# Attention with the inverse sums folded into the matrix that turns the probabilities, multiplied in float32

## The chip, the core and the metric

The kernel runs on one core of a Trainium2 chip. TensorE (PE in the rows, with its weight loads as PEld) multiplies matrices, VectorE is DVE, ScalarE is ACT, GpSimd is POOL, and SyncE (SP) issues transfers. The metric is the device time of one execution in microseconds (us), the median of several runs.

## What is computed

One layer of a hybrid decoder on 1024 positions of width 1024: a gated feed-forward block, a mixer with two branches (a recurrence and an attention), and a second feed-forward block. The change touches only the attention, whose core is this, for 8 heads and queries in blocks of 128:

```python
def attend(i):
    start = i * Q_BLOCK
    qn = lax.dynamic_slice_in_dim(q_nope, start, Q_BLOCK, axis=1)
    qr = lax.dynamic_slice_in_dim(q_rope, start, Q_BLOCK, axis=1)
    sc = jnp.einsum('bqhd,bkhd->bhqk', qn, k_nope) + jnp.einsum('bqhr,bkr->bhqk', qr, k_rope)
    sc = sc.astype(jnp.float32) * scale
    causal = k_idx[None, :] <= (start + jnp.arange(Q_BLOCK))[:, None]
    sc = jnp.where(causal[None, None], sc, -jnp.inf)
    p = jax.nn.softmax(sc, axis=-1).astype(v.dtype)
    return jnp.einsum('bhqk,bkhd->bqhd', p, v)
```

## The kernel before

Every large product is made of three matmuls on operands that are split into a high part and a low part (`mm3`, lines 88 to 90; ScalarE makes the high part at line 94, VectorE the low part at line 98). In the trace these operands stand as f32 or fp32r.

The attention works through 64 steps n, eight query tiles s = 0 to 7 for each of eight heads h. Step n has the scores of 128 queries against the (s + 1) x 128 keys that they may see. Every engine has its own instruction queue, written out in the order of the steps, and semaphores tie the queues together:

- `scores` (TensorE): three matmuls for each piece of up to 512 keys and one bfloat16 matmul that adds the causal mask (line 2245). Scores of step n go to one of two pairs of PSUM banks, so scores n wait for the exponentials of step n - 2.
- `maximum` (VectorE, line 2256) and `exponent` (ScalarE, line 2266, which also leaves the row sum in `rs`). The exponentials go to one of three buffers of `probs`.
- `normalise` (GpSimd): line 2272 raises the 128 sums to the power -1, and line 2275 multiplies the whole of `prob(n)`, 128 x (s + 1) x 128, by them in place.
- `turn` (TensorE, line 2290) transposes the s + 1 blocks of 128 x 128 of `prob(n)` through the identity into PSUM bank 4 (the first four blocks, piece 0) and bank 5 (the others, piece 1). The program calls it two steps late: the queue has scores n and then turn n - 2. There is one bank for each piece, so `turn` of a step waits until VectorE has taken the same piece of the step before (`pt_split`).
- `turned_hi` (ScalarE, line 94) and `turned_lo` (VectorE, line 98) split the turned blocks into `a_pt`.
- `product` (TensorE, line 2322) multiplies the turned probabilities by the values once for four query tiles. ScalarE (`take`, line 2338) and VectorE (`add`, line 2343) bring the result into `a_o`.
- Beside steps 1 and 7 of even heads, and 1, 3, 6 and 7 of odd heads, a `unit` projects the queries or keys of a later head (`unit_of`, 9 or 6 matmuls of 512 columns, rows `ps<-cq,w` and `ps<-ckv,w`). VectorE multiplies two parts of a query unit by the rotation's tables (lines 2188 and 2189) and splits the rest (2191), GpSimd adds the two parts (`rope_pool`, line 2207, in its queue behind `normalise` of the step), ScalarE takes the sum (line 2175), and its exponentials of the next step stand behind that in its queue.

A head has 1 + 2 + ... + 8 = 36 blocks to turn, so the kernel turns 288. The work repeats with a period of two heads, since the units differ for even and odd heads; scores of even heads have 96 rows, those of odd heads 128.

Of the kernel before, what the change touches and what calls it, by code (L numbers as in the profile page):

```python
# [19 lines left out]
ALU = mybir.AluOpType  # L20
# [3 lines left out]
P = 128  # L24
# [27 lines left out]
BASE = 16512  # L52
# [4 lines left out]
AT_AREA = AT_U + 65536  # L57
# [6 lines left out]
class Core:  # L64


    def __init__(self, nc, ctx):
        self.nc, self.ctx = nc, ctx
        self.ps = ctx.enter_context(nc.psum_tensor("ps", [P, 8, HALF], F32))
        self.squared = None  # L70
# [166 lines left out]
class TileNorm:  # L237
# [118 lines left out]
    def turn(self, pe, t, b, bank_free=None):  # L356
        pe.wait_ge(self.S["gained_r"], self.pres + t + 1)
        if bank_free is not None:
            pe.wait_ge(self.S["u_split"], self.split_count(bank_free))
        for k in range(DK):  # L360
            last = pe.transpose(self.c.ps[:, b + k // 4, (k % 4) * P:(k % 4 + 1) * P],  # L361
                                self.work(t)[:, k * P:(k + 1) * P], self.c.ident[:, :])
        last.then_inc(self.S["turned"], 1)
# [1616 lines left out]
class Attention:  # L1980
# [6 lines left out]
    def __init__(self, c, w, lat, w_uq, w_ukv):  # L1987
        self.c, self.nc, self.w, self.lat = c, c.nc, w, lat
        names = ("v_done", "v_hi", "v_lo", "zero", "kr_hi", "kr_split", "kr_copied", "unit_done", "q_hi", "q_rot", "q_sum", "rope_hi", "q_split",
                 "k_hi", "u_dve", "s_done", "max_done", "p_done", "norm_done", "t_done", "pt_hi", "pt_split", "o_done",  # L1990
                 "o_aux", "o_add", "o_hi", "o_split")
        self.S = {n: c.sem("a_" + n) for n in names}
        vq = w_uq.rearrange("(k p) (h e) -> p k h e", p=P, h=HEADS)
        vkv = w_ukv.rearrange("(k p) (h e) -> p k h e", p=P, h=HEADS)
        self.n_v = w.new(KC * HEADS * VH)
        for k in range(KC):
            w.piece(self.n_v, w.raw_of(self.n_v)[:, k * HALF:(k + 1) * HALF].rearrange("p (h e) -> p h e", e=VH),
                    vkv[:, k, :, NOPE:NOPE + VH])
        self.n_a = []
        half = ROPE // 2  # L2000
        for h in range(HEADS):
            n = w.new(QC * P + (0 if h % 2 else KC * P))
            q = w.raw_of(n)[:, 0:QC * P].rearrange("p (k f) -> p k f", f=P)
            even = ((0, QK, 0), (QK, half, NOPE + half), (QK + half, half, NOPE))
            odd = ((0, half, NOPE + half), (half, half, NOPE), (ROPE, ROPE, NOPE), (NOPE, NOPE, 0))
            for to, width, at in odd if h % 2 else even:
                w.piece(n, q[:, :, to:to + width], vq[:, :, h, at:at + width])
            if h % 2 == 0:
                for k in range(KC):
                    w.piece(n, w.raw_of(n)[:, (QC + k) * P:(QC + k + 1) * P].rearrange("p (h e) -> p h e", e=NOPE),  # L2010
                            vkv[:, k, h:h + 2, 0:NOPE])
            self.n_a.append(n)
        u = AT_U
        self.pt_hi, self.pt_lo = (c.at(u + 16384 * i, f"a_pt{i}", [P, 8, 4, P], F32R) for i in range(2))
        self.q_hi, self.q_lo = ([c.at(u + 32768 + 4096 * (2 * par + i), f"a_q{par}{i}", [P, SEQ], F32R) for par in range(2)]
                                for i in range(2))
        k_at = (u + 49152, u + 57344, AT_AREA + 73728)
        self.k_hi, self.k_lo = ([c.at(at + 4096 * i, f"a_k{n}{i}", [P, SEQ], F32R) for n, at in enumerate(k_at)] for i in range(2))
        self.v = c.at(AT_AREA + 40960, "a_v", [P, HEADS, NT, P], F32R)
        self.rot, self.rot2 = c.at(AT_AREA + 81920, "a_rot", [P, HALF]), c.at(AT_AREA + 100352, "a_rot2", [P, HALF])  # L2020
        self.probs = c.at(AT_AREA + 83968, "a_probs", [P, 3, SEQ])
        self.o = c.at(AT_AREA + 96256, "a_o", [P, SEQ])
        self.o_lo3 = c.at(AT_AREA + 36864, "a_o_lo3", [P, SEQ], F32R)
        self.neg, self.rs, self.inv = (c.at(BASE + 2400 + 64 * i, f"a_s{i}", [P, 16]) for i in range(3))
        self.scale = float(QK) ** -0.5

        self.units = [("q", 0, 0), ("k", 0, 0), ("q", 0, 1), ("k", 0, 1)]
        for h in range(HEADS - 1):
            if h % 2:
                self.units += [("k", (h + 1) // 2, 0), ("q", h + 1, 0), ("k", (h + 1) // 2, 1), ("q", h + 1, 1)]  # L2030
            else:
                self.units += [("q", h + 1, 0), ("q", h + 1, 1)]
        self.index = {unit: i for i, unit in enumerate(self.units)}
        self.closes = [self.index[("k", 0, 1)]] + [self.index[("q", h, 1)] for h in range(1, HEADS)]
# [231 lines left out]
        self.nc.scalar.activation(self.prob(n), self.seen(n), ACT.Exp, bias=self.neg[:, i:i + 1], scale=1.0,  # L2266
                                  accum_out=self.rs[:, i:i + 1]).then_inc(self.S["p_done"], 1)

    def normalise(self, pool, n):
        i = n % 16  # L2270
        pool.wait_ge(self.S["p_done"], n + 1)
        self.nc.gpsimd.tensor_tensor(self.inv[:, i:i + 1], self.rs[:, i:i + 1], self.c.expo[:, 1:2], ALU.pow)\
            .then_inc(self.S["norm_done"], 1)
        pool.wait_ge(self.S["norm_done"], 2 * n + 1)
        self.nc.gpsimd.tensor_scalar(self.prob(n), self.prob(n), self.inv[:, i:i + 1], 1.0, ALU.mult, ALU.mult)\
            .then_inc(self.S["norm_done"], 1)

    def turn(self, pe, n):
        c, s = self.c, n % HEAD_TILES
        pe.wait_ge(self.S["norm_done"], 2 * n + 2)  # L2280
        if n == 0:
            pe.wait_ge(self.S["u_dve"], 4)
        for b in self.pieces(n):
            if b == 0 and n > 0:
                pe.wait_ge(self.S["pt_split"], self.piece(n - 1, 0) + 1)
            if b == 1 and n >= HEAD_TILES or b == 1 and s > 4:
                pe.wait_ge(self.S["pt_split"], self.piece(n - 1 if s > 4 else n - 5, 1) + 1)
            for j in range(4 * b, min(4 * b + 4, s + 1)):
                at = s - j if b else j
                last = pe.transpose(c.ps[:, 4 + b, at * P:(at + 1) * P], self.prob(n)[:, j * P:(j + 1) * P], c.ident[:, :])  # L2290
            last.then_inc(self.S["t_done"], 1)

    def turned(self, x, n, b):
# [105 lines left out]

    def pool_step(self, pool, n):  # L2400
        if n > 0 and self.beside(n - 1):
            pool.wait_ge(self.S["norm_done"], 2 * n)
            self.rope_pool(pool, self.beside(n - 1))
        self.normalise(pool, n)

    def pe_step(self, pe, n):
        h, s = n // HEAD_TILES, n % HEAD_TILES
# [236 lines left out]
def hybrid_layer(nc, a, out):  # L2644
# [6 lines left out]
    with ExitStack() as ctx:  # L2651
# [47 lines left out]
        with nc.Block() as block:  # L2699
# [522 lines left out]
            def _(pe):  # L3222
# [8 lines left out]
                for q in range(NT):  # L3231
                    turn(f1, q)
# [77 lines left out]
                for g in range(3):  # L3310
                    for k in range(DK - 2):
                        op.chunk_of(pe, g, k)
                        if g > 0:
                            for s, q in out_steps(g, k):
                                if s == 5:
                                    if q == 0:
                                        op.evacuated(pe, 1)
                                    turn(f2, q)
                    op.tail_of(pe, g)
                turn(f2, 5)  # L3320
                op.evacuated(pe, 6)
                turn(f2, 6)
# [31 lines left out]
```

## Time and profile before

| | us |
|---|---|
| median of 3 runs | 2243.08 |
| lowest and highest | 2242.76 and 2245.47 |
| the profiled execution, its own time | 2243.93 |
| its span in the trace | 2242.1 |
| TensorE busy in the span | 2152.5 (96%) |
| VectorE, ScalarE, GpSimd busy | 1368.2, 979.4, 405.5 |
| the 64 steps of the attention in it | from 1244 to 1456 |

The profiled execution's own time is 1.8 us above its span, and its span covers first to last instruction. Times in rows are in microseconds from the start of the span, unless a column says ns. Matmuls are pipelined: the duration of one contains its latency, and what a further one costs is the distance between two starts.

### The profile page before, as it was taken

Reading aid. Unit: us, or ns where it says so; the run is one execution under the profiler, and the core shown is the slowest. Engines: PE = TensorE matmul, PEld = TensorE weight load, DVE = VectorE, ACT = ScalarE, POOL = GpSimd, SP = SyncE. Lnnn points to the kernel's source line nnn. Section 1 sums busy time; section 2 is a strip of 40 time slices with the busy share of each in tenths; the row PEclk is TensorE's granted clock in tenths of the full one; section 3 lists DMA queues with packets and bytes.
Section 4 is the critical chain, followed back from the end, with each engine's and each line's share of the span. In section 5 each row is a group of like instructions: output and inputs, shape, how many; then the busy total and the mean of one; then the engine's idle time right before and its main releaser. Section 6 shows DMA issues by size and latency. Waiting matters only on the chain.

```text
span 2242.1 us, 25934 instructions
## 1 busy us (share of the span) xinstructions
PE 2152.5 (96%) x9837; PEld 1787.4 (80%) x9837; DVE 1368.2 (61%) x1719; ACT 979.4 (44%) x1559; POOL 405.5 (18%) x444
## 2 busy tenths in 40 slices
PE   5999999999998999999999888899899999999998
PEld 4888788878886888888888677788788888888886
DVE  7667865557585665311212788677856766547666
ACT  6443333334362777411323666535533333333444
POOL 3123320000032122000011455402213331000012
PEclk9999999999999999999999999999999999999999
DMA  3355442252442211222411100255335453216234
GB/s 122 95 171 188 154 165 71 71 202 94 151 159 80 52 48 47 66 76 69 124 44 38 29 10 10 104 194 209 105 98 192 166 192 126 69 50 230 94 137 155
DMA packets 220293, 249.85 MB, mean 111 GB/s; under 512 B 24261, under 2 KB 161546, under 8 KB 220170
## 3 DMA queue, kind: packets, MB, share of 16 engines
q1 hardware_dynamic: 220170, 248.19, 33.7%
q8 instruction: 79, 1.29, 0.2%
q14 instruction: 44, 0.36, 0.1%
HBM read 192.06 MB, written 55.57 MB: 110 GB/s over the span
## 4 chain that ended last, share of the span: by engine, by line
PE 88%; DVE 5%; ACT 2%; issue 2%; POOL 1%; DMA 0%; SPq 0%; POOLq 0%; ACTq 0%; DVEq 0%
PE ps L88 29%; PE ps L89 28%; PE ps L90 28%; PE ps L2322 1%; PE ps L2290 1%; PE ps L361 1%; POOL a_rot L2207 1%; ACT a_probs L2266 1%; DVE a_pt L98 0%; DVE a_s L2256 0%; DVE entry_y L346 0%; DVE a_rot L2189 0%; DVE a_rot L2188 0%; DMA entry_x<-in_x_dram 0%; ACT w_hi L94 0%
## 5 line engine op out<-in xcount | busy, mean ns | idle before, releaser
L98 DVE TENSOR_TENSOR ff_w_lo<-ff_raw,ff_w_hi 128x512 fp32r<-128x512 f32 x264 | 211.7, 805 | 172.5 <-ACT ff_w_hi L94 172.1
L89 PE MATMUL ps<-ff_t,ff_w_hi 128*128 128x512 f32 x704 | 273.9, 389 | 0.0
L90 PE MATMUL ps<-ff_t,ff_w_lo 128*128 128x512 f32 x704 | 273.9, 389 | 0.0
L88 PE MATMUL ps<-ff_t,ff_w_hi 128*128 128x512 f32 x704 | 273.9, 389 | 0.0
L94 ACT ACTIVATE ff_w_hi<-ff_raw 128x512 fp32r<-128x512 f32 x264 | 164.7, 627 | 177.4 <-PE ps L90 172.7
L88 PE MATMUL ps<-d_b_hi,d_a_hi 128*128 128x512 f32 x608 | 237.5, 391 | 3.8 <-DVE d_a_lo L98 3.7
L90 PE MATMUL ps<-d_b_hi,d_a_lo 128*128 128x512 f32 x608 | 236.6, 389 | 0.0
L89 PE MATMUL ps<-d_b_lo,d_a_hi 128*128 128x512 f32 x608 | 236.6, 389 | 0.0
L98 DVE TENSOR_TENSOR w_lo<-w_raw,w_hi 128x1024 fp32r<-128x1024 f32 (+2 forms) x81 | 90.5, 1119 | 235.0 <-ACT w_hi L94 235.0
L88 PE MATMUL ps<-ff_b,ff_w_hi 128*128 128x512 f32 x528 | 208.5, 395 | 6.0 <-ACT ff_u2x L696 5.0
L89 PE MATMUL ps<-ff_b,ff_w_hi 128*128 128x512 f32 x528 | 207.7, 393 | 0.0
L90 PE MATMUL ps<-ff_b,ff_w_lo 128*128 128x512 f32 x528 | 207.5, 393 | 0.0
L88 PE MATMUL ps<-u_hi,w_hi 128*128 128x512 f32 x512 | 200.8, 392 | 2.4 <-DVE u_lo L98 2.4
L89 PE MATMUL ps<-u_lo,w_hi 128*128 128x512 f32 x512 | 200.2, 391 | 0.0
L90 PE MATMUL ps<-u_hi,w_lo 128*128 128x512 f32 x512 | 200.1, 391 | 0.0
L88 PEld LDWEIGHTS ps<-ff_t,ff_w_hi 128*128 128x128 f32 x704 | 132.3, 188 | 27.6
L89 PEld LDWEIGHTS ps<-ff_t,ff_w_hi 128*128 128x128 f32 x704 | 132.2, 188 | 27.5
L90 PEld LDWEIGHTS ps<-ff_t,ff_w_lo 128*128 128x128 f32 x704 | 132.2, 188 | 27.3
L94 ACT ACTIVATE w_hi<-w_raw 128x1024 fp32r<-128x1024 f32 (+2 forms) x81 | 78.3, 968 | 152.6 <-PE ps L90 145.2
L88 PEld LDWEIGHTS ps<-d_b_hi,d_a_hi 128*128 128x128 f32 x608 | 114.2, 188 | 29.4 <-DVE d_a_lo L98 6.1
L90 PEld LDWEIGHTS ps<-d_b_hi,d_a_lo 128*128 128x128 f32 x608 | 114.1, 188 | 23.8
L89 PEld LDWEIGHTS ps<-d_b_lo,d_a_hi 128*128 128x128 f32 x608 | 114.2, 188 | 23.3
(301 smaller groups left out, 4312.1 us busy)
## 6 DMA issues: line engine op xcount, KB each, us to landing
ff_raw<-in_ffn_w_gate_dram SPq DMA_DIRECT2D x44, 512.0 KB, 3.9
ff_raw<-in_ffn_w_up_dram SPq DMA_DIRECT2D x44, 512.0 KB, 3.9
d_sums<-in_ffn_w_down_dram SPq DMA_DIRECT2D x44, 512.0 KB, 4.1
sums_scratch<-d_sums SPq DMA_DIRECT2D x88, 256.0 KB, 2.6
w_raw<-in_w_in_dram SPq DMA_DIRECT2D x32, 512.0 KB, 4.0
d_raw<-sums_scratch SPq DMA_DIRECT2D x24, 512.0 KB, 3.2
w_raw<-in_w_out_dram SPq DMA_DIRECT2D x24, 512.0 KB, 3.9
spill_scratch<-ff_st SPq DMA_DIRECT2D x44, 256.0 KB, 3.0
```

Source lines behind the costliest of these rows:

```text
L88: pe.matmul(out, lh, rh, start=start, stop=False, skip_group_check=go_on)
L89: pe.matmul(out, lh, rl, start=False, stop=False, skip_group_check=go_on)
L90: return pe.matmul(out, ll, rh, start=False, stop=stop, skip_group_check=go_on)
L94: return nc.scalar.activation(hi, src, ACT.Copy)
L98: return nc.vector.tensor_tensor(lo, src, as_f32(hi), ALU.subtract)
L361: last = pe.transpose(self.c.ps[:, b + k // 4, (k % 4) * P:(k % 4 + 1) * P], self.work(t)[:, k * P:(k + 1) * P], self.c.ident[:, :])
L2207: self.nc.gpsimd.tensor_tensor(self.rot[rope, :], self.rot[rope, :], self.rot2[rope, :], ALU.add)\
L2266: self.nc.scalar.activation(self.prob(n), self.seen(n), ACT.Exp, bias=self.neg[:, i:i + 1], scale=1.0, accum_out=self.rs[:, i:i + 1]).then ...
L2290: last = pe.transpose(c.ps[:, 4 + b, at * P:(at + 1) * P], self.prob(n)[:, j * P:(j + 1) * P], c.ident[:, :])
L2322: last = pe.matmul(c.ps[:, 6, first * P:HALF], self.v[:, h, j, :], pt[:, unit, first:4, :].rearrange("p b q -> p (b q)"), start=j + i == 0 ...
```

## The change

GpSimd no longer touches the exponentials. It multiplies the 128 x 128 identity by the inverse sums, which gives a diagonal matrix (`shares`, three buffers in turn). TensorE then turns the unscaled exponentials by an ordinary matmul against that diagonal in place of a transpose against the identity. `prob(n)` stays the operand that is loaded as weights, and the diagonal is the one that streams. Both are float32 and the new instruction is `pe.matmul`, not `pe.transpose`. The semaphore `norm_done`, raised twice in a step, becomes `inv_done` and `share_done`, each raised once. `turn` waits for `share_done`.

```diff
-    def normalise(self, pool, n):
+    def share(self, pool, n):
         i = n % 16
         pool.wait_ge(self.S["p_done"], n + 1)
         self.nc.gpsimd.tensor_tensor(self.inv[:, i:i + 1], self.rs[:, i:i + 1], self.c.expo[:, 1:2], ALU.pow)\
-            .then_inc(self.S["norm_done"], 1)
-        pool.wait_ge(self.S["norm_done"], 2 * n + 1)
-        self.nc.gpsimd.tensor_scalar(self.prob(n), self.prob(n), self.inv[:, i:i + 1], 1.0, ALU.mult, ALU.mult)\
-            .then_inc(self.S["norm_done"], 1)
+            .then_inc(self.S["inv_done"], 1)
+        pool.wait_ge(self.S["inv_done"], n + 1)
+        self.nc.gpsimd.tensor_scalar(self.shares[n % 3][:, :], self.c.ident[:, :], self.inv[:, i:i + 1], 1.0, ALU.mult, ALU.mult)\
+            .then_inc(self.S["share_done"], 1)
 
     def turn(self, pe, n):
...
-        pe.wait_ge(self.S["norm_done"], 2 * n + 2)
+        pe.wait_ge(self.S["share_done"], n + 1)
...
-                last = pe.transpose(c.ps[:, 4 + b, at * P:(at + 1) * P], self.prob(n)[:, j * P:(j + 1) * P], c.ident[:, :])
+                last = pe.matmul(c.ps[:, 4 + b, at * P:(at + 1) * P], self.prob(n)[:, j * P:(j + 1) * P], self.shares[n % 3][:, :], start=True, stop=True)
```

The order on the engines stays. On TensorE, at the first two steps of an odd head, the queue before has the last score matmuls of step 0 of that head, the turn of tile 6 of the head before, the scores of step 1, the turn of tile 7, and then a unit:

```order
L2245 MATMUL ps<-mask_b,ident_b 128x128
L2290 MATMUL ps<-ident,a_probs 128x128 x7
L88 MATMUL ps<-a_k_172,a_q_167 128x256
L89 MATMUL ps<-a_k_175,a_q_167 128x256
L90 MATMUL ps<-a_k_172,a_q_169 128x256
L2245 MATMUL ps<-mask_b,ident_b 128x128
L2290 MATMUL ps<-ident,a_probs 128x128 x8
L88 MATMUL ps<-ckv_106,w_hi 128x512
```

The same place in the changed kernel, where line 2292 is the new matmul:

```order
L2246 MATMUL ps<-mask_b,ident_b 128x128
L2292 MATMUL ps<-a_shares_186,a_probs 128x128 x7
L88 MATMUL ps<-a_k_172,a_q_167 128x256
L89 MATMUL ps<-a_k_175,a_q_167 128x256
L90 MATMUL ps<-a_k_172,a_q_169 128x256
L2246 MATMUL ps<-mask_b,ident_b 128x128
L2292 MATMUL ps<-a_shares_187,a_probs 128x128 x8
L88 MATMUL ps<-ckv_106,w_hi 128x512
```

Nothing moved there; only the kind of the 7 and 8 instructions and their streamed operand are different. On GpSimd, at the end of an even head, the queue before is this (`a_s_184` are the inverse sums):

```order
L2275 TENSOR_SCALAR a_probs<-a_probs,a_s_184 128x896
L2272 TENSOR_TENSOR a_s_184<-a_s_183,expo 128x1
L2275 TENSOR_SCALAR a_probs<-a_probs,a_s_184 128x1024
L2207 TENSOR_TENSOR a_rot<-a_rot,a_rot_178 32x512
L2272 TENSOR_TENSOR a_s_184<-a_s_183,expo 128x1
```

And in the changed kernel, where lines 2274, 2277 and 2208 are what 2272, 2275 and 2207 were:

```order
L2277 TENSOR_SCALAR a_shares_185<-ident,a_s_184 128x128
L2274 TENSOR_TENSOR a_s_184<-a_s_183,expo 128x1
L2277 TENSOR_SCALAR a_shares_186<-ident,a_s_184 128x128
L2208 TENSOR_TENSOR a_rot<-a_rot,a_rot_178 32x512
L2274 TENSOR_TENSOR a_s_184<-a_s_183,expo 128x1
```

The sequence is the same, and every multiplication is 128 columns wide.

## Rows read from the trace of the kernel before

**Rows 1.** The page's busy times: us (share of the span) xinstructions.
```profile
PE 2152.5 (96%) x9837; PEld 1787.4 (80%) x9837; DVE 1368.2 (61%) x1719; ACT 979.4 (44%) x1559; POOL 405.5 (18%) x444
```

**Rows 2.** Table by stretch: one round of two heads; busy us, clock, DMA.
```profile
1303.50:1354.90 51.40, 45.17 (x258) 37.76 (x257) 42.83 (x68) 34.83 (x75) 26.96 (x37) 0.97 0.04 11
```

**Rows 3.** Waits in that round: who waited for whom, us, times, longest us.
```profile
PE ps L2290 <- DVE a_pt L98: 5.8, 4, 1.8
ACT a_q L2175 <- POOL a_rot L2207: 5.6, 4, 1.9
...
PEld ps L2290 <- POOL a_probs L2275: 0.2, 1, 0.2
```

**Rows 4.** Groups, 1240 to 1460: xcount, busy us, mean ns, idle before.
```profile
L2290 PE MATMUL ps<-ident,a_probs 128*128 128x128 f32 x288 | 45.9, 289 | 22.4 <-DVE a_pt L98 21.9 <-POOL a_probs L2275 0.3
...
L2275 POOL TENSOR_SCALAR a_probs<-a_probs,a_s 128x1024 f32<-128x1024 f32 x8 | 9.0, 1121 | 0.8
...
L2275 POOL TENSOR_SCALAR a_probs<-a_probs,a_s 128x128 f32<-128x128 f32 x8 | 3.0, 374 | 0.8
```

**Rows 5.** Timeline of TensorE, around four turns: start us, us, idle before.
```profile
1308.39 0.52 PE L2290 MATMUL ps<-ident,a_probs 128*128 128x128 f32 x3 [1.47 <-DVE a_pt L98]
...
1319.79 0.93 PE L2290 MATMUL ps<-ident,a_probs 128*128 128x128 f32 x7
...
1322.94 1.06 PE L2290 MATMUL ps<-ident,a_probs 128*128 128x128 f32 x8 [1.80 <-DVE a_pt L98]
...
1335.87 0.63 PE L2290 MATMUL ps<-ident,a_probs 128*128 128x128 f32 x4 [1.01 <-DVE a_pt L98]
...
1336.86 0.50 PE L88 MATMUL ps<-a_k,a_q 128*128 128x512 f32 x1 [0.36 <-ACT a_probs L2266]
...
1349.16 1.06 PE L2290 MATMUL ps<-ident,a_probs 128*128 128x128 f32 x8 [1.55 <-DVE a_pt L98]
```

**Rows 6.** Lines 2290 (a transpose) and 1424 (plain float32, one column): records, ns min/median/max.
```profile
L2290 PE MATMUL ps<-ident,a_probs x288: 270/273/447, 1251.0 to 1450.9; 128*128 128x128 f32 x144
...
L1424 PEld LDWEIGHTS ps<-t_one,t_freq_rows x4: 181/186/187, 112.0 to 112.3; 1*128 1x128 f32 x4
L1424 PE MATMUL ps<-t_one,t_freq_rows x4: 245/245/266, 112.0 to 112.3; 1*128 1x1 f32 x4
```

**Rows 7.** Timeline of TensorE: neighbours of 256 and of 512 columns.
```profile
1347.14 0.28 PE L89 MATMUL ps<-a_k,a_q 96*128 96x256 f32 x1
1347.26 0.28 PE L90 MATMUL ps<-a_k,a_q 96*128 96x256 f32 x1
...
1317.59 0.39 PE L89 MATMUL ps<-cq,w_hi 128*128 128x512 f32 x1
1317.82 0.40 PE L90 MATMUL ps<-cq,w_lo 128*128 128x512 f32 x1
```

**Rows 8.** Timeline of the other engines on the way to the turn at 1322.94.
```profile
1319.64 0.68 DVE L2188 TENSOR_TENSOR a_rot<-ps,trig 32x512 f32<-32x512 f32 x1 [0.41 <-PE ps L90]
...
1320.27 1.12 POOL L2275 TENSOR_SCALAR a_probs<-a_probs,a_s 128x1024 f32<-128x1024 f32 x1
...
1320.35 0.68 DVE L2189 TENSOR_TENSOR a_rot<-ps,trig 32x512 f32<-32x512 f32 x1
...
1320.43 0.98 ACT L94 ACTIVATE a_pt<-ps 128x512 fp32r<-128x512 f32 x2 [0.20 <-PE ps L2290]
...
1321.47 1.25 POOL L2207 TENSOR_TENSOR a_rot<-a_rot,a_rot 32x512 f32<-32x512 f32 x1
...
1322.11 1.16 DVE L98 TENSOR_TENSOR a_pt<-ps,a_pt 128x512 fp32r<-128x512 f32 x2
```

**Rows 9.** Table by stretch: three of the four at a granted clock near 0.50.
```profile
1252.00:1262.30 10.30, 8.82 (x35) 6.91 (x34) 5.65 (x10) 5.51 (x13) 5.15 (x9) 0.54 0.47 85
1309.20:1312.60 3.40, 3.40 (x14) 2.90 (x13) 2.40 (x5) 1.78 (x5) 2.66 (x4) 0.50 0.00 0
...
1411.60:1418.40 6.80, 6.80 (x26) 5.74 (x25) 4.50 (x6) 3.07 (x8) 4.41 (x6) 0.50 0.00 1
```

More of the change, by code:

```diff
@@ L1989, in __init__ @@
         names = ("v_done", "v_hi", "v_lo", "zero", "kr_hi", "kr_split", "kr_copied", "unit_done", "q_hi", "q_rot", "q_sum", "rope_hi", "q_split",
-                 "k_hi", "u_dve", "s_done", "max_done", "p_done", "norm_done", "t_done", "pt_hi", "pt_split", "o_done",
+                 "k_hi", "u_dve", "s_done", "max_done", "p_done", "inv_done", "share_done", "t_done", "pt_hi", "pt_split", "o_done",
                  "o_aux", "o_add", "o_hi", "o_split")
@@ L2024, in __init__ @@
         self.neg, self.rs, self.inv = (c.at(BASE + 2400 + 64 * i, f"a_s{i}", [P, 16]) for i in range(3))
+        self.shares = [c.at(at, f"a_shares{i}", [P, P]) for i, at in enumerate((AT_AREA + 102400, AT_AREA + 102912, BASE + 1440))]
         self.scale = float(QK) ** -0.5
@@ L2401, in pool_step @@
         if n > 0 and self.beside(n - 1):
-            pool.wait_ge(self.S["norm_done"], 2 * n)
+            pool.wait_ge(self.S["share_done"], n)
             self.rope_pool(pool, self.beside(n - 1))
-        self.normalise(pool, n)
+        self.share(pool, n)
     def pe_step(self, pe, n):
```

## Prediction

> **What bounds the kernel now.** I read the page's busy times first: TensorE is busy for 96% of the span, with VectorE next at 61% [rows 1]. Time added to TensorE is therefore added to the kernel unless it falls into one of TensorE's gaps. So the second view is the table by stretch for the part that the change touches. The steps of the attention repeat every two heads, in a round of 51.4 us. In it TensorE is busy for 45.2 us and idle for 6.2, VectorE busy for 42.8, ScalarE for 34.8 and GpSimd for 27.0 [rows 2]. Third, the waits of that round say where the gaps are: four waits of `turn` for VectorE's `a_pt`, 5.8 us together, while `turn` waited for GpSimd's multiplication for 0.2 us only [rows 3]. Over all 64 steps it is 21.9 us against 0.3 on the matmul [rows 4]. The engine that the change relieves is hardly waited for, and the one that it loads is the bound.
>
> **GpSimd: what is taken away.** One multiplication takes 1121 ns for 1024 columns and 374 ns for 128 [rows 4]. All become 374 ns, and a step with s = 7 saves 0.75 us. This lies beside other work. `turn` runs two steps late, so the scaled data is there long before it is asked for, except for the 0.2 us in a round [rows 3]. The other one who waits for GpSimd is ScalarE, for the rotation's sum, 5.6 us in a round [rows 3]. Of the four sums only those at the end of a head stand right behind a long multiplication: at 1320.27 it takes until 1321.39, and the sum starts at 1321.47, though line 2189 had left its second input at 1321.03. So ScalarE may have its sum 0.4 us earlier there [rows 8]. Who profits? The exponentials of step 0, which TensorE needs only at step 2, behind the turn of eight blocks and a unit. I take 0.3 us off the whole kernel for this and for the 0.3 above, and bound it by 0 and 2 us.
>
> **TensorE: what one turned block costs.** Today seven blocks take 0.93 us from the first start to the last end, and one alone lasts 0.27 [rows 6], so a further block costs (0.93 - 0.27)/6 = 0.11 us; eight give (1.06 - 0.27)/7 = 0.113. I use 0.112 [rows 5]. The new instruction is a plain float32 matmul, and the trace of before has this kind in one place only: two such instructions of one column, which stand as four records, each with its weight load [rows 6]. A transpose has one record: 288 for 288 blocks [rows 4]. So I expect 576 records. The four are spread over 0.3 us, hence some 0.11 us apart with nothing to stream: a record costs at least 0.11, which its weight load seems to set, and a block at least 0.224. With 128 columns to stream there may be more. If each record streams its 128 columns twice, the nearest row is a matmul of 256 columns, which follows its neighbour after 0.12 us [rows 7]. Then a block costs 0.24. If each streams them four times, the nearest row is one of 512 columns, 0.23 us [rows 7], and a block costs 0.46. I take 0.24, since it lies next to the bound that was measured on this kind of instruction. A block costs 0.128 us more than now, with 0.112 as the lower end and 0.35 as the upper.
>
> The Trainium skill ("FP8 and Floating Point Precision", TensorE Precision Notes) says of true float32 that it takes four passes through the array. Two records of two passes each would agree with that, and the trace shows the two records. Four passes of 128 columns as one stream of 512 would come to 0.23 us a block by the spacing above, and the sum below would be about 2 us smaller.
>
> All blocks together: 288 x 0.128 = 36.9 us of TensorE's time, 9.2 us for the 72 blocks of a round.
>
> **What of it falls into gaps.** I follow a round turn by turn; its turns have 2, 3, 4, 5, 6, 7, 8, 1, 2, 3, 4, 5, 6, 7, 8 and 1 blocks. A longer turn is hidden where a gap follows whose end does not depend on it.
> - The gap of 1.80 us ahead of the turn of eight at 1322.94 [rows 5]. Its end is set by VectorE: the unit's end releases line 2188 at 1319.64, three instructions of the unit and a maximum follow, then `a_pt` at 1322.11 [rows 8]. The turn of seven at 1319.79 lies inside that stretch. ScalarE's part of it ends at 1321.41 now, 0.7 us ahead of VectorE's start, and piece 0 shifts by 4 x 0.128 = 0.5. So seven blocks, 0.9 us, are hidden. The gap of 1.55 ahead of 1349.16 is alike: seven more.
> - The gap of 1.47 us ahead of 1308.39 hides the turns of one and two blocks before it: ScalarE and VectorE are busy with other work there. Three blocks.
> - The gap of 1.01 us ahead of 1335.87 is again the end of a unit followed by VectorE's queue, and the turn of three lies inside. Three blocks. Then scores wait 0.36 us for exponentials that are behind the rotation's sum [rows 5], which hides 0.36 of the next turn.
> - The turns of eight (0.90 us becomes 1.92) are followed by a unit and scores with no gap. The product behind them also needs VectorE's split of these turns; no wait of it is among the waits of the round, and TensorE's longer turn makes it come later itself. All the others (3, 4, 5, 6, then 5 and 6) run without a gap into the next unit.
>
> Hidden: 20 blocks x 0.128 + 0.36 = 2.9 us of 9.2 in a round, so 6.3 stay. Four rounds: 36.9 - 4 x 2.9 = 25.3. The last head has no units and shallower gaps, the first one has deeper ones; I leave these against each other. With 0.112 the same count gives 32.3 - 10.4 = 21.9. With nothing hidden, because ScalarE and VectorE get each turned piece later by the same amount, it is 36.9.
>
> **The clock.** Four stretches, 23.9 us together, ran at a granted clock near 0.50, which is 1.2 instead of 2.4 GHz. The one that [rows 9] leaves out is like the second and one round later. The last three came right behind the gap ahead of a turn of three, and TensorE was busy throughout them [rows 9]. Each costs half its length: 1.7, 1.7 and 3.4 us. In the changed kernel TensorE does more and idles less just ahead of them, so I expect that half of this comes back, 3.4 us. The first stretch follows gaps of the attention's start, which stay, and its turns of 2, 3 and 4 cost double there: 9 x 0.128 = 1.2 us more. Net -2.2, between -12 (all four gone) and +5 (all stay and one more comes).
>
> The Trainium skill ("TensorE: Matmul & The Clock Gate", Part 4: PE-mode transpose) says that a transpose doesn't count as activity for the clock gate as a matmul does. By it the replacement alone would keep the clock up. No row here separates the two, since transposes always stand between matmuls.
>
> **The sum.** 25.3 - 2.2 - 0.3 = +22.8 us on the profiled execution's 2243.93, which is 2266.7. The median of the runs is 0.85 lower, so I forecast 2266 us.
>
> **The rivals.**
> - Nothing hides: the split of the turned pieces is itself on the path, as in VectorE's 42.8 busy us of 51.4 [rows 2]. +36.9 and the clock as it is now, with 1.2: about 2281. Against it: the gaps are ended by units, by the rows above.
> - The clock stays high: all three later stretches go, and most of the first (its busy 8.8 us [rows 9] halved is 4.4). 25.3 - 6.8 - 4.4 = +14: about 2257. For it: TensorE is denser. Against: the gaps of 1.47 shrink to 1.1 and don't vanish.
> - The expensive block: each record costs 0.23, as 512 columns do, or as a load and a stream that don't overlap (0.11 + 0.12). 288 x 0.348 = 100; the gaps take what they can, some 5.8 a round, 23 in all. +77: about 2320. Against it: loads are hidden behind streams in every row here.
> - The block costs what it costs now: one record of 0.112, since the two records of [rows 6] would be a peculiarity of that line. Then only 0.3 us of GpSimd's moves: 2243.
> - Faster: the same cheap block, and the clock of the three later stretches comes back: 2243.1 - 6.8 = 2236. It decides only if a block costs less than 6.8/208 = 0.03 us more than now, 208 being the 288 blocks less the 80 that are hidden. The 0.11 between records speaks against it.
>
> **How the numbers follow.** The forecast has 0.57, nothing hidden 0.15, the high clock 0.15, the expensive block 0.06, the same cost 0.04, faster 0.03. The range reaches from the high clock with the lower price (21.9 - 6.8 - 4.4 = +10.7, 2254) to nothing hidden with one more stretch at half clock (36.9 + 1.2 + 3.4 = +41.5, 2285), and leaves out the last three cases and a little. What a measurement of this kernel can tell from no change is about 0.2%, 4.5 us: faster 0.03, within it 0.04, slower 0.93.
>
> **What would show it.** Line 2292 should have 576 records of TensorE, pairs some 0.24 us apart; eight blocks should take about 2 us where they took 1.06. 288 records would break the first step, pairs 0.46 apart the price. A round should last 57 to 58 us instead of 51.4, and the four waits for `a_pt` in it should shrink from 5.8 us to about 3.3; if they stay at 5.8, nothing was hidden. GpSimd's 64 multiplications should all take 374 ns, and TensorE should gain nothing by it. The granted clock after the turns of two and three blocks tells the last term. Outside the attention nothing should move.

## The result, and the profile after

| | before | after |
|---|---|---|
| median, us | 2244.27 (4 runs) | 2263.07 (4 runs) |
| lowest and highest, us | 2242.76 to 2247.39 | 2261.90 to 2263.80 |
| span of the profiled execution, us | 2242.1 | 2260.8 |

The ratio is 1.0086, with a 95% interval from 1.0074 to 1.0099: slower by 18.8 us. The forecast was 2266 us, or +22.8 on the profiled execution, whose span grew by 18.7.

The new matmul is two records, as in [rows 6]: 576 of them for 288 blocks, where [rows 4] has 288. One line's view of the kernel after (records, ns min/median/max, first and last start):

```profile
L2292 PEld LDWEIGHTS ps<-a_shares,a_probs x576: 186/192/353, 1249.7 to 1469.4; 128*128 128x128 f32 x192
L2292 PE MATMUL ps<-a_shares,a_probs x576: 270/275/581, 1249.7 to 1469.5; 128*128 128x128 f32 x192
```

The timeline of TensorE in the kernel after, at the places of [rows 5] and at the next two turns behind the turn of three (start us, us, idle before). A turn of k blocks stands as 2k records:

```profile
1301.75 2.02 PE L2292 MATMUL ps<-a_shares,a_probs 128*128 128x128 f32 x16 [0.70 <-DVE a_pt L98]
...
1313.15 0.91 PE L2292 MATMUL ps<-a_shares,a_probs 128*128 128x128 f32 x6 [0.99 <-DVE a_pt L98]
...
1315.52 1.13 PE L2292 MATMUL ps<-a_shares,a_probs 128*128 128x128 f32 x8 [0.33 <-DVE a_pt L98]
...
1318.15 1.35 PE L2292 MATMUL ps<-a_shares,a_probs 128*128 128x128 f32 x10 [0.20 <-DVE a_pt L98]
...
1329.07 2.02 PE L2292 MATMUL ps<-a_shares,a_probs 128*128 128x128 f32 x16 [0.95 <-DVE a_pt L98]
...
1343.32 1.13 PE L2292 MATMUL ps<-a_shares,a_probs 128*128 128x128 f32 x8 [0.62 <-DVE a_pt L98]
...
1358.01 2.02 PE L2292 MATMUL ps<-a_shares,a_probs 128*128 128x128 f32 x16 [0.70 <-DVE a_pt L98]
```

Sixteen records take 2.02 us and one alone 0.275, so they follow each other after (2.02 - 0.275)/15 = 0.116 us. A block is two records and costs 0.233 us, where it cost 0.112: 0.121 more, 34.8 us for 288 blocks. The gaps ahead of the turns of eight fell from 1.80 and 1.55 us to 0.95 and 0.70, that ahead of the turn of three from 1.47 to 0.99. Two gaps are new, 0.33 and 0.20 us, ahead of the turns of four and five.

The table by stretch, for one round and for the attention behind its first steps (busy us of TensorE, its weight loads, VectorE, ScalarE and GpSimd, then the granted clock), and the waits of that round:

```profile
1301.70:1358.00 56.30, 52.39 (x328) 45.37 (x329) 42.93 (x68) 35.39 (x76) 20.93 (x36) 1.00 0.04 10
...
1262.40:1455.00 192.60, 179.28 (x1129) 155.26 (x1128) 144.21 (x228) 119.95 (x257) 71.45 (x125) 1.00 0.11 37
```

```profile
PE ps L2292 <- DVE a_pt L98: 3.8, 6, 1.0
ACT a_q L2176 <- POOL a_rot L2208: 3.5, 5, 1.7
```

Against [rows 2] the round is 4.9 us longer. TensorE is busy for 7.2 us more (52.39 against 45.17) and idle for 2.3 us less (3.9 against 6.2). VectorE does the same work. GpSimd does 6 us less in a round, and ScalarE waits for it for 3.5 us instead of 5.6 [rows 3]; whether TensorE gains by that is the question of the second experiment. All of the three later stretches at half clock [rows 9] are gone from this execution; the first is still there.

**Where the 18.7 us are.** The starts of the turns of eight cut the attention into one piece for each head. The table takes them from the timelines of the two profiled executions.

| piece (us) | before | after | change |
|---|---|---|---|
| first scores to the turn of eight of head 0 | 27.75 | 30.14 | +2.39 |
| head 1 | 26.22 | 28.95 | +2.73 |
| head 2 (a half-clock stretch before) | 25.03 | 27.32 | +2.29 |
| head 3 | 26.22 | 28.94 | +2.72 |
| head 4 (a half-clock stretch before) | 25.09 | 27.32 | +2.23 |
| head 5 | 26.24 | 28.96 | +2.72 |
| head 6 (the long half-clock stretch before) | 26.79 | 27.46 | +0.67 |
| head 7 | 22.83 | 25.99 | +3.16 |
| to the last product | 5.01 | 5.98 | +0.97 |

The sum is +19.9 us. The stages ahead, which have the same instructions in both, took 1.3 us less in the execution after (first scores at 1242.66 against 1243.94). That makes 18.6 of 18.7. (The start of the first scores moves by as much between two executions of one and the same kernel, that of experiments six and seven: 1243.02 and 1244.39.)

### The profile page after: what moved, and what is told of

It is laid out like the page before. It is cut to its first block, busy times and chain, and to the rows that moved or that the text cites. A ratio compares the mean times of both kernels' runs of the same rounds, so it can differ in the third digit from the quotient of the medians.

```text
span 2260.8 us, 26510 instructions
## 1 busy us (share of the span) xinstructions
PE 2180.9 (96%) x10125; PEld 1817.6 (80%) x10125; DVE 1367.9 (61%) x1719; ACT 981.2 (43%) x1559; POOL 381.3 (17%) x444
## 4 chain that ended last, share of the span: by engine, by line
PE 90%; DVE 5%; ACT 2%; issue 2%; POOL 1%; DMA 0%; SPq 0%; POOLq 0%; ACTq 0%; DVEq 0%
PE ps L88 29%; PE ps L90 28%; PE ps L89 28%; PE ps L2292 3%; PE ps L2324 1%; PE ps L361 1%; DVE a_pt L98 1%; DVE entry_y L346 0%; DMA entry_x<-in_x_dram 0%; DVE a_s L2257 0%; DVE a_rot L2190 0%; DVE a_rot L2189 0%; ACT a_pt L94 0%; POOL a_rot L2208 0%; ACT w_hi L94 0%
```

## The experiments

Every kernel is the kernel before with the edit shown, unless the text says otherwise, and was compared with the kernel before on the same chip.

**One: TensorE's part alone.**

```diff
-                last = pe.transpose(c.ps[:, 4 + b, at * P:(at + 1) * P], self.prob(n)[:, j * P:(j + 1) * P], c.ident[:, :])
+                last = pe.matmul(c.ps[:, 4 + b, at * P:(at + 1) * P], self.prob(n)[:, j * P:(j + 1) * P], c.ident[:, :], start=True, stop=True)
```

> TensorE's part alone: GpSimd still multiplies all columns as before, and TensorE turns the blocks with plain float32 matmuls against the identity. Theory (the new matmul is the whole cost): as the changed kernel, 1.0085 of the time before or +19 us, 576 records about 0.116 us apart, and the same granted clock as in the changed kernel. Rival (GpSimd's narrower work bought back some us in the changed kernel): this kernel is 3 us or more slower than the changed one.

Measured: 2263.01 us against 2242.62, ratio 1.0092 (1.0077 to 1.0107), and 576 records. The changed kernel had 2263.07. The clock was full in the attention behind the first stretch, too, and the pieces between its turns of eight are those of the changed kernel to 0.14 us each. TensorE's part alone gives the whole cost, within the noise.

**Two: GpSimd's part alone.** The changed kernel with the transpose kept. The diagonal is made but not used, so this kernel leaves out the division by the sums:

```diff
-                last = pe.matmul(c.ps[:, 4 + b, at * P:(at + 1) * P], self.prob(n)[:, j * P:(j + 1) * P], self.shares[n % 3][:, :], start=True, stop=True)
+                last = pe.transpose(c.ps[:, 4 + b, at * P:(at + 1) * P], self.prob(n)[:, j * P:(j + 1) * P], c.ident[:, :])
```

> GpSimd's part alone: GpSimd makes the diagonal of 128 columns as in the changed kernel, but TensorE transposes against the identity as before, so the probabilities are not divided by their sums. Theory (nobody on the path waits for GpSimd): within 1 us of before, GpSimd busy for 24 us less in the attention, and the three stretches at half clock still there. Rival (the rotation's sum is on the path): 2 to 4 us faster.

Measured: 2242.27 us against 2242.62, ratio 0.9996 (0.9987 to 1.0005). TensorE's gaps are those of [rows 5] to 0.04 us, three of them here:

```profile
1309.10 0.52 PE L2292 MATMUL ps<-ident,a_probs 128*128 128x128 f32 x3 [1.43 <-DVE a_pt L98]
...
1323.70 1.06 PE L2292 MATMUL ps<-ident,a_probs 128*128 128x128 f32 x8 [1.80 <-DVE a_pt L98]
...
1336.56 0.63 PE L2292 MATMUL ps<-ident,a_probs 128*128 128x128 f32 x4 [1.01 <-DVE a_pt L98]
```

The times alone would allow a gain of up to 2.9 us. The trace is narrower. It has the three later stretches at half clock as well, the last one shorter (about 3.5 us instead of 6.8), which makes head 6 faster by 1.57 us. The other pieces of the table above are together 0.3 us shorter. So taking 23 us of work off GpSimd (106.6 against 83.2 us in the attention) is worth 0.3 us or nothing.

**Three and four: which blocks hide.** Plain matmuls in the 20 blocks of a round that the prediction took as hidden, or in the other 52:

```diff
+                if s == 6 or (n // HEAD_TILES % 2 == 0 and s < 2) or (n // HEAD_TILES % 2 == 1 and s == 2):
+                    last = pe.matmul(c.ps[:, 4 + b, at * P:(at + 1) * P], self.prob(n)[:, j * P:(j + 1) * P], c.ident[:, :], start=True, stop=True)
+                else:
+                    last = pe.transpose(c.ps[:, 4 + b, at * P:(at + 1) * P], self.prob(n)[:, j * P:(j + 1) * P], c.ident[:, :])
```

The second kernel has `not (...)` around the same condition.

> Plain float32 matmuls against the identity only in the 20 blocks of a round that the count took as hidden in gaps (the turns of seven, those of one and two blocks in even heads, that of three in odd heads), transposes in the other 52; GpSimd as before. 80 blocks x 0.121 = 9.7 us more TensorE time. Theory (they are hidden): no cost, and if the clock of the three later stretches comes back as well, up to 6.8 us faster than before. Rival (nothing hides, the split of the turned pieces is the path): +9.7 us less what the clock gives, so +3 to +10 us.

> The complement: plain float32 matmuls against the identity in the 52 blocks of a round that the count took as on the path, transposes in the 20 hidden ones; GpSimd as before. 208 x 0.121 = 25.2 us more TensorE time. Theory (the count is right): all of it is on the path, less what the clock gives back; with the three stretches back at the full clock it is about as slow as with all 72 blocks, +18 to +21 us. Rival (a longer turn is hidden anywhere in part): +14 us or less.

Measured: 20 blocks, 2243.86 us, ratio 1.0000 (0.9991 to 1.0009). The other 52, 2263.41 us against 2243.03, ratio 1.0087 (1.0072 to 1.0103). So 80 blocks of 0.121 us, 9.7 us of TensorE's time, left the time where it was, and the other 208 cost as much as all 288 do. The table by stretch for a round of each, the one with 20 blocks first:

```profile
1296.60:1347.40 50.80, 46.35 (x277) 38.94 (x278) 42.59 (x68) 35.04 (x75) 26.79 (x37) 1.00 0.04 12
```

```profile
1302.30:1358.60 56.30, 49.87 (x309) 42.86 (x309) 42.92 (x68) 35.15 (x76) 26.87 (x36) 1.00 0.04 11
```

The times alone don't settle the first half, since the profiled execution with the 20 blocks has one later stretch at half clock (near 1411) and the kernel before has three. Its gaps settle it. In a round at the full clock they are shorter by what the turns ahead of them grew:

```profile
1296.57 1.06 PE L2293 MATMUL ps<-ident,a_probs 128*128 128x128 f32 x8 [0.70 <-DVE a_pt L98]
1307.06 0.52 PE L2293 MATMUL ps<-ident,a_probs 128*128 128x128 f32 x3 [1.04 <-DVE a_pt L98]
...
1321.10 1.06 PE L2293 MATMUL ps<-ident,a_probs 128*128 128x128 f32 x8 [0.95 <-DVE a_pt L98]
1334.04 0.63 PE L2293 MATMUL ps<-ident,a_probs 128*128 128x128 f32 x4 [0.63 <-DVE a_pt L98]
```

And the round takes 50.80 us from turn of eight to turn of eight, against 50.76 in a round at the full clock without any plain matmul (shown below, in the part on the clock). One place was not hidden: the turn of seven in the last head. Its piece is 23.72 us long, against 22.83 in the kernel before, so 0.8 us or so of the 9.7 were paid there.

The round with the other 52 blocks is as long as that of the changed kernel, 56.30 us, while TensorE is busy for 2.5 us less: 20 x 0.121 = 2.4. Its gaps show where that time is instead:

```profile
1302.30 2.02 PE L2291 MATMUL ps<-ident,a_probs 128*128 128x128 f32 x16 [1.55 <-DVE a_pt L98]
1313.70 0.91 PE L2291 MATMUL ps<-ident,a_probs 128*128 128x128 f32 x6 [1.43 <-DVE a_pt L98]
...
1329.61 2.02 PE L2291 MATMUL ps<-ident,a_probs 128*128 128x128 f32 x16 [1.80 <-DVE a_pt L98]
```

These are the gaps of the kernel before [rows 5]. Where the cheap transposes stay in the hidden turns, a longer wait follows them and nothing is gained.

**Five: is it the plain matmul that brings the clock back?**

```diff
+                pe.transpose(c.ps[:, 4 + b, at * P:(at + 1) * P], self.prob(n)[:, j * P:(j + 1) * P], c.ident[:, :])
                 last = pe.transpose(c.ps[:, 4 + b, at * P:(at + 1) * P], self.prob(n)[:, j * P:(j + 1) * P], c.ident[:, :])
```

> Every transpose is issued twice into the same place, so that a block costs about as much TensorE time as in the changed kernel (2 x 0.112 against 0.233 us) but all of it in transposes. Theory A (the clock of the three stretches came back because TensorE works longer and idles less there): these stretches run at the full clock here as well, and the time is about 1.5 us below the changed kernel, +17 us. Theory B (it came back because a plain matmul counts for the clock gate and a transpose doesn't): the stretches at half clock stay or grow, and the time is 5 us or more above that, +22 us or more.

Measured: 2260.21 us against 2242.62, ratio 1.0077 (1.0063 to 1.0091), 17.6 us slower. The table by stretch for the attention behind its first steps:

```profile
1262.40:1450.00 187.60, 173.03 (x1113) 149.07 (x1112) 142.71 (x225) 118.43 (x253) 90.65 (x123) 1.00 0.10 33
```

The clock was full although every block was turned by transposes. By the sentence of the Trainium skill that the prediction draws on ("TensorE: Matmul & The Clock Gate", Part 4: PE-mode transpose), the change of the kind of instruction would be what keeps the clock up; here the clock came back without it. How much a transpose counts stays open, since score and unit matmuls stand between the turns in every kernel.

The mean granted clock of whole executions says the same of more than one trace. It was 0.991 or 0.992 in all 16 executions of the changed kernel and of the kernels of experiments one, four and five, and 0.987 to 0.990 in the 57 executions of the kernel before that were measured beside the experiments. One stretch of 3.4 us moves this mean by less than 0.001, so it doesn't exclude a single one.

**Six to eleven: what the clock hangs on.** Two edits, alone and together. The first doubles the transposes only for `s in (0, 1)`. The second puts m more matmuls ahead of the attention's first unit (m = 8 or 4):

```diff
+                if s in (0, 1):
+                    pe.transpose(c.ps[:, 4 + b, at * P:(at + 1) * P], self.prob(n)[:, j * P:(j + 1) * P], c.ident[:, :])
...
+        for _ in range(8 if i == 0 else 0):
+            pe.matmul(c.ps[:, bank, :], self.w.both(n, slice(first * P, (first + 1) * P))[0], x[0][:, 0, half_of(hf)], start=True, stop=True)
```

The doubling alone:

> Only the turns of one and two blocks are made of doubled transposes (24 blocks, 2.7 us of TensorE time, half of it in the gap that was 1.47 us). It asks how little more work ahead of the turn of three keeps the clock. Theory (activity ahead of it decides): one or more of the three stretches go, and the time is 0 to 3 us below before. Rival (what decides is when the stretch falls, by the time at which the attention starts): the same three stretches, perhaps shifted, and 1 us slower.

Measured: 2240.53 us against 2243.03, ratio 0.9988 (0.9979 to 0.9997), and no later stretch at half clock in the profiled execution. That looked like a kernel that beats both, so the same kernel ran once more:

> The kernel with doubled transposes in the turns of one and two blocks once more, since 0.9988 of the time before is near what can be told apart. If the clock's gain is a property of the kernel, 1.5 to 3.5 us faster again and no stretch at half clock between the first of the attention and the one behind it; if it was an accident of that run, within 1 us.

Measured: 2241.71 against 2242.23, ratio 0.9998 (0.9989 to 1.0007), and one stretch at half clock in its profiled execution, from 1412 to 1416. By the expectation the gain was an accident of the first run. It is not shown to be faster. Its clock is another matter: the mean granted clock was 0.991 or 0.992 in 15 of the 22 executions of both sets, a value that none of the kernel before reached. So the doubling keeps the clock more often, not always, and gains no time that can be told from noise.

Eight matmuls ahead, without the doubling:

> Eight more matmuls of 512 columns ahead of the first unit of the attention, overwritten by the unit's own, so everything after starts about 1.8 us later with the same work and gaps. It parts the clock's place from its cause. If the activity in the gaps alone decides, the stretches at half clock come at the same turns, 1.8 us later, and the time is +1.8 us. If their coming depends on how the gaps lie in time, they move to other turns, or are missing in some rounds, and the time is +1.8 us less 1.0 to 1.7 for each that goes.

Measured: 2245.23 against 2243.03, ratio 1.0011 (1.0001 to 1.0020). The attention started at 1247.14, 3.2 us later than in the kernel before and not 1.8, with one more stretch at half clock just ahead of it (1241 to 1245). In its profiled execution the clock is halved in two later stretches, and not at the turns of before. The table by stretch has parts of them, and the last round's place, where the kernel before has its longest:

```profile
1310.80:1314.00 3.20, 2.70 (x15) 2.22 (x16) 3.06 (x4) 1.79 (x5) 2.07 (x3) 0.88 0.02 4
1314.20:1317.40 3.20, 3.20 (x14) 2.56 (x14) 1.49 (x2) 1.75 (x4) 2.23 (x3) 0.62 0.00 0
1365.40:1372.00 6.60, 6.60 (x27) 5.72 (x26) 3.04 (x5) 3.59 (x8) 3.46 (x6) 0.56 0.00 0
1416.00:1424.00 8.00, 7.21 (x42) 5.84 (x43) 6.14 (x9) 5.71 (x13) 5.24 (x8) 1.00 0.03 9
```

The turn of three stood at 1310.78 and that of four at 1313.15, so the first of these began a turn later than in the kernel before. The last round has none.

Four matmuls ahead, without the doubling, and four and eight with it, one execution each:

> Before with four extra matmuls ahead of the attention and no doubled transposes, 0.9 us later. If the gaps of the kernel before are at the edge, stretches at half clock come in some of the three rounds and not in others, as with eight.

> The same with four extra matmuls, 0.9 us later: a third place in time. Activity: no later stretch. Timing: one or more of them.

> The doubled transposes in the turns of one and two blocks, and the eight extra matmuls ahead of the attention. If more activity ahead of the turn of three keeps the clock wherever the gaps fall, there is no later stretch at half clock here either. If the doubled transposes only moved the gaps in time, stretches come back as they did with the eight matmuls alone.

Measured: four without the doubling, 2241.56 us and one later stretch, near 1360. Four with it, 2242.61 us and none. Eight with it, 2248.6 us and three. Two of the stretches of the last one, and the attention of the one with four:

```profile
1325.80:1329.00 3.20, 3.20 (x14) 2.56 (x14) 1.58 (x3) 1.76 (x5) 1.59 (x4) 0.67 0.02 5
1366.80:1370.00 3.20, 3.20 (x15) 2.62 (x15) 1.85 (x3) 1.70 (x6) 1.81 (x3) 0.68 0.00 0
```

```profile
1262.40:1455.00 192.60, 168.43 (x989) 140.08 (x988) 152.99 (x241) 126.70 (x275) 97.01 (x131) 1.00 0.11 37
```

The kernel before and the five kernels of this part (six profiled executions, since one ran twice) have nearly the same work and gaps in a round. In the order of the text they had three, none, one, two, one, none and three later stretches. More activity ahead of the turn of three doesn't reliably keep the clock: with the doubling there were none, one, none and three. That the place of the gaps in time decides is not shown. The traces fit it, but one kernel had none in one execution and one in another, so with a single trace of each kernel chance between executions fits as well. Whether the changed kernel always keeps the clock by its fuller rounds wasn't settled. The four kernels with more TensorE work on the path (the changed one, and those of the experiments one, four and five) were nearly free of it: three had no later stretch, the fourth (the 52 blocks) one near 1429.

**Twelve: the price of a record.** Each block by two matmuls of 64 columns:

```diff
+                for e in (0, P // 2):
+                    last = pe.matmul(c.ps[:, 4 + b, at * P + e:at * P + e + P // 2], self.prob(n)[:, j * P:(j + 1) * P],
+                                     c.ident[:, e:e + P // 2], start=True, stop=True)
```

> Each block is turned by two plain float32 matmuls of 64 columns against the halves of the identity: 1152 records that stream half as many columns each. If the record's 0.117 us is set by its stream of 128 columns taken twice, a record costs less here, at least the 0.11 that line 1424 showed with one column; if the weight load sets it, it stays at 0.11 to 0.117, and a block costs 0.45 us. In both cases TensorE has some 62 us more than in the changed kernel, and the whole is 2315 to 2325 us.

Measured: 2318.82 us in one run. The timeline of its TensorE at a turn of eight:

```profile
1318.51 3.74 PE L2291 MATMUL ps<-ident,a_probs 128*128 128x64 f32 x32
```

(3.74 - 0.275)/31 = 0.112 us for a record that streams 64 columns, against 0.116 with 128. Half the columns save 0.004 us, so it is not the stream that sets the 0.112 us. A fixed cost of a record does; that this is its weight load is likely but was not separated from other fixed costs. A stream of 128 float32 columns lies only just above this floor.

## Why the prediction was right

**The bound, and who waits for GpSimd.** Both held. The first two experiments put the whole change on TensorE (1.0092) and nothing that can be told from noise on GpSimd (0.9996); the 0.3 us that the forecast gave it agrees with the pieces of the second experiment but is too small to be shown. One detail was off: not all 64 multiplications took 374 ns. Their mean is 409 ns. Eight of them, about one for each head, took longer (0.93 us twice, 0.69 to 0.75 three times, 0.45 three times), and each of the eight lay beside a split of a weight on VectorE. Rows of the kernel after, the group and that moment:

```profile
L2277 POOL TENSOR_SCALAR a_shares<-ident,a_s 128x128 f32<-128x128 f32 x64 | 26.1, 409 | 6.3
```

```profile
1336.56 0.83 DVE L98 TENSOR_TENSOR w_lo<-w_raw,w_hi 128x640 fp32r<-128x640 f32 x1 [1.04 <-ACT w_hi L94]
1336.69 0.93 POOL L2277 TENSOR_SCALAR a_shares<-ident,a_s 128x128 f32<-128x128 f32 x1
```

**The price of a block.** Two records, as forecast from line 1424. The price was 0.233 us, and the forecast 0.24; the lower bound of 0.224 was closer to the mark than the row of 256 columns that I took. That is 34.8 us for all blocks instead of 36.9. The four passes that the Trainium skill names ("FP8 and Floating Point Precision", TensorE Precision Notes), taken as one stream of 512 columns, would have given 0.23; the trace agrees with that number, though not with one stream, since a block is two records.

**What hides.** The list of hidden turns was right in all rounds but for the turn of seven of the last head, which cost about 0.8 us. In the kernel with plain matmuls in these 20 blocks the gaps shrank by what the turns ahead grew, 0.85 us where seven blocks cost 7 x 0.121. In the changed kernel the 1.47 us gap fell by 0.48 for three blocks, and the wait of 0.36 us went. The four waits for `a_pt` came to 3.3 us, as forecast; with two new ones, of which below, they are 3.8. The round took 56.3 us, where 57 to 58 had been expected.

**The clock.** Here a term was mis-sized twice, and the errors went against each other. I let half of the three later stretches come back, and all did. But I priced each of them at half of its length, 1.7 us. The table of pieces shows less. A head without a stretch can be seen in the kernel with four matmuls ahead (experiment nine; its line 2292 is the transpose, its line 2277 GpSimd's multiplication), whose turns of eight at both ends of a round and three turns between them stand here:

```profile
1297.07 1.06 PE L2292 MATMUL ps<-ident,a_probs 128*128 128x128 f32 x8 [1.55 <-DVE a_pt L98]
...
1307.55 0.52 PE L2292 MATMUL ps<-ident,a_probs 128*128 128x128 f32 x3 [1.48 <-DVE a_pt L98]
1309.92 0.63 PE L2292 MATMUL ps<-ident,a_probs 128*128 128x128 f32 x4 [0.50 <-POOL a_probs L2277]
1312.05 0.74 PE L2292 MATMUL ps<-ident,a_probs 128*128 128x128 f32 x5 [0.21 <-DVE a_pt L98]
...
1347.83 1.06 PE L2292 MATMUL ps<-ident,a_probs 128*128 128x128 f32 x8 [1.55 <-DVE a_pt L98]
```

From the turn of three to the turn of five it takes 4.50 us. In the kernel before the same way runs at half clock:

```profile
1310.85 1.06 PE L2290 MATMUL ps<-ident,a_probs 128*128 128x128 f32 x4
...
1313.42 0.74 PE L2290 MATMUL ps<-ident,a_probs 128*128 128x128 f32 x5
```

It takes 5.03 us there (1308.39 [rows 5] to 1313.42), only 0.53 us more, though it has none of the waits: its matmuls take 0.53 + 0.71 = 1.2 us longer. At the full clock TensorE comes to the turns of four and five too early and waits 0.50 and 0.21 us. (For the first, GpSimd's data were last in this execution; in the kernel with the doubling alone the same 0.50 us ends with VectorE's split, so the two are close together there.) The whole pieces say the same. At the full clock that of an even head takes 24.5 us (24.52 and 24.53 in two kernels), against 25.03 and 25.09 in the kernel before, and that of head 6 takes 24.75 against 26.79. So a short stretch at half clock cost 0.5 us and the long one 2 us, 3 us together instead of 6.8. The forecast had 3.4 of them come back. The right amount came from a wrong price times a wrong share, which is luck.

The price hangs on the place. In the execution with eight matmuls ahead and the doubling, one short stretch lies over a turn of eight and the unit behind it, where no wait follows soon:

```profile
1324.38 1.83 PE L2294 MATMUL ps<-ident,a_probs 128*128 128x128 f32 x8 [1.80 <-DVE a_pt L98]
```

The turn takes 1.83 us instead of 1.06, and the piece 28.08 us, where it takes 26.46 without a stretch. That is 1.6 us, close to half of the stretch, as the prediction had priced it.

**The sum by its terms, with what was measured.** 34.8 for the blocks. Less what hid: four rounds of 20 x 0.121 + 0.36 = 2.8, which is 11.1. Less 3 for the clock, plus 1 for the turns in the first stretch, an estimate from nine blocks of 0.121 us at half clock. Less 1.3 for the stages ahead, which is within what two executions of one kernel differ by. That makes 20.4, and the span has 18.7. The other 1.7 us are time that hid outside the list, 1.3 of them in the three rounds from head 1 to head 6. The clean round of the kernel with four matmuls ahead is 50.76 us (1297.07 to 1347.83) and that of the changed kernel 56.26, so 5.5 of 8.7 us stayed, where the list leaves 5.9. The new waits of 0.50 and 0.21 us of the full clock are gaps too, and the longer turns of three and four fill a part of them (0.33 and 0.20 are left). The gap ahead of the turn of three took 0.1 us more than its three blocks. Against the forecast of 22.8 us, the lower price took off 1.6, the further hidden time 1.7 and the stages ahead 1.3; the clock came out 0.2 us higher, and the 0.3 us given to GpSimd is not in this sum.

**The rivals.** Nothing hides (2281) and the expensive block (2320) fell by the table and the records. The kernel with two matmuls for each block came to 2318.82, because there a block does cost 0.45 us; the sum that gave 2320 for that price came out near in this one run, whose first stretch at half clock was longer (until 1273, not 1260), so the agreement is in part chance. The cheap block, and with it the faster kernel (2236), fell with the 576 records. The high clock (2257) was half right: the three later stretches went, but were worth 3 us and not 6.8, and the first stretch, to which it gave 4.4 us, stayed.

## What to carry to other kernels

Folding a scale into a transposition through a diagonal looks free, since a matmul takes the place of a matmul. In float32 it is not: for a block of 128 x 128 the plain matmul runs as two records of 0.116 us where the transpose is one of 0.112. Before moving work from an idle engine to the bound one, look for who waits for the idle one; here TensorE waited for GpSimd for 0.2 us in a round of 51.

When a step grows, go through its places one by one: a place ahead of a gap whose end another engine sets takes the growth for nothing, and two kernels that change the complementary places test such a list. And a stretch at a low clock can be worth far less than half of its length, where the full clock runs into waits that the low one had covered: 0.5 us in one place and 1.6 in another, for stretches of about 3.4 us.

## What the hardware showed that I had not expected

- A plain float32 matmul against 128 columns costs 0.233 us and has two records of 0.116; against 64 columns a record still costs 0.112.
- Stretches at half clock came and went between kernels with nearly the same work and gaps (three, two, one or none behind the first of the attention), and between two executions of one kernel (none and one). The three of the kernel before cost 3 us. Its executions differ by more than that, from 2240.67 to 2246.69 us in one set, and the execution with four matmuls ahead and the doubling took 2242.61 us without any of them. So a gain of 0.1% needs more than one set of runs: 0.9988 in one was 0.9998 in the next.
- A GpSimd instruction of 128 columns took 0.45 to 0.93 us instead of 0.37 in the eight cases in which it lay beside VectorE's split of a weight from SBUF to SBUF, and in no other.
